# Seeding the last output group in PSUM, a shorter chain to the last root, and smaller stores

## The chip, the cores and the metric

The kernel runs on one core of one Trainium2 chip. The metric is the time of one execution on the device in microseconds (us), as the median of several runs. Engines are called PE (TensorE, matrix products), DVE (VectorE), ACT (ScalarE), POOL (GpSimd) and SP (SyncE, which only issues transfers here). SBUF is the on-chip memory, PSUM the accumulators that PE writes into, 8 banks of 512 float32 columns on 128 partitions.

## What is computed

Two layers over x (256 rows of 2048 features, float32): a gated differential attention, then a gated Conformer convolution, each added to x, and one RMSNorm at the end. Only the last lines matter here:

```
# layer 1, the convolution's output projection, with its bias
y = (u * silu(z)) @ w_out + b_out            # [256, 2048] @ [2048, 2048] + [2048]
x = x + y
# the final norm
out = x * rsqrt(mean(x * x, axis=-1) + 1e-6) * final_gain
```

## The kernel before

The program is one block with a hand-written instruction stream for each engine; semaphores tie them together, and nothing is reordered by a scheduler. float32 products are made of three fast ones: each operand is split into a high part (ScalarE copies it to the type float32r) and a low part (the rest), and `project` issues hi x hi, hi x lo and lo x hi for every 128-row slice of the contraction.

Weights come in chunks of 4 slices by 512 columns (1 MB) through a ring of 4 slots. For each chunk SP loads `w_raw`, ACT writes `w_hi` (L422) once PE has freed the slot (`w_free`), and the low part `w_lo` is made by DVE in the first part of the program and by POOL from chunk `POOL_FROM` on (L413), so in the whole output projection of the convolution. Four chunks make one group of 512 output columns (`GW`); `PAIRS` is 4, so w_out has the groups n = 0 to 3. `acc` has 4 banks: group n uses the banks 2*(n%2) and 2*(n%2)+1, one for each row tile st (rows 0 to 127, and 128 to 255). A group is 96 products: 4 chunks, 4 slices, 2 row tiles, 3 products.

The end of the program, around which the change lies, runs so on each engine:

- DVE, loop over n = 0 to 3: add the output bias to the residual in `xs` (L982, both row tiles: two operands in SBUF, result in SBUF). Then for n < 3: wait until PE has finished group n, add `acc` to `xs` (L990), wait for ACT's sum of squares, and multiply by the final gain (L995, again two operands in SBUF). For n = 3, once for each row tile: add `acc` (L1004), multiply by the gain into `gained_rows` (L1006), add up the four sums of squares (L1009), scale and add epsilon (L1010), wait for ACT's root, take the reciprocal (L1013), scale the column groups 0 and 1 (L1017).
- ACT: high parts of the chunks (L422), the squares of each finished group with a sum (L685, `squares_of_y`), and at the end for each row tile the root (L697) and the scaling of the groups 2 and 3 (L701).
- PE: the groups 0 to 2 with both row tiles in each chunk, where group n >= 2 waits for `y_ready` (the banks emptied by DVE). Group 3 is written out apart: first all four chunks for row tile 0, then all four for row tile 1, so that the end of row tile 0 runs beside the products of row tile 1. The first product of a bank has `start=True`, which overwrites; the others add to what the bank holds.
- SP: the stores of the output, two for each row tile, 1024 columns (512 KB) each (L387).

The waits of group 3 on PE before:

```
pe.wait_ge(y_ready, 2 * (PAIRS - 2))
for st in range(ST):
    for i in range(NCH):
        if st == 0:
            low_part_ready(pe, CHUNKS - NCH + i)
```

Of the kernel before, what the change touches and what calls it, by code (L numbers as in the profile page):

```python
# [21 lines left out]
F32 = mybir.dt.float32  # L22
# [4 lines left out]
P = 128  # L27
# [48 lines left out]
def build(nc, x, x_turned, vectors, taps, final_gain, rel_bias, attn_w_in, attn_w_out, conv_w_in,  # L76
          conv_w_out, conv_b_out, onehot, out):
    with ExitStack() as ctx:  # L78
# [74 lines left out]
        with ExitStack() as one:  # L153
            b_out_bc = sb("b_out_bc", [P, D], F32, one)
            gain_bc = sb("gain_bc", [P, D], F32, one)
            gained_rows = sb("gained_rows", [P, ST, GW], F32, one)
            junk = sb("junk", [P, ST, GW], F32, one)
# [159 lines left out]
        def _(sp):  # L317
# [66 lines left out]
            for st in range(ST):  # L384
                for ready, cols in ((out_ready, slice(0, D // 2)), (out_ready_act, slice(D // 2, D))):
                    sp.wait_ge(ready, 2 * (st + 1))
                    sp.dma_start(out_rows[:, st, cols], xs[:, st, cols]).then_inc(out_stored, 16)  # L387
            sp.wait_ge(out_stored, 16 * PAIRS)
# [29 lines left out]
        def _(act):  # L418
# [269 lines left out]
            for i in range(NCH * PAIRS):  # L688
                if i:
                    hi_of(CHUNKS_CONV + i + RING)  # L690
                if i % NCH == NCH - 1 and i < NCH * (PAIRS - 1):
                    for st in range(ST):
                        squares_of_y(i // NCH, st)
            for st in range(ST):
                squares_of_y(PAIRS - 1, st)
                act.wait_ge(ms_ready, 3 + st)
                act.activation(sd[:, st:st + 1], ms[:, st:st + 1], ACT.Sqrt).then_inc(sd_ready, 1)  # L697
                act.wait_ge(rstd_ready, 4 + st)
                for n in (2, 3):
                    src = xs[:, st, n * GW:(n + 1) * GW] if n < PAIRS - 1 else gained_rows[:, st]  # L700
                    act.activation(xs[:, st, n * GW:(n + 1) * GW], src, ACT.Copy, scale=rstd[:, st:st + 1]  # L701
                                   ).then_inc(out_ready_act, 1)


        @block.vector
        def _(dve):
# [270 lines left out]

            dve.wait_ge(final_landed, 32)
            for n in range(PAIRS):
                for st in range(ST):  # L980
                    cols = xs[:, st, n * GW:(n + 1) * GW]
                    dve.tensor_tensor(cols, cols, b_out_bc[:, n * GW:(n + 1) * GW], ALU.add  # L982
                                      ).then_inc(y_ready_pre, 1)
                if n == PAIRS - 1:
                    break
# [12 lines left out]

            n = PAIRS - 1
            dve.wait_ge(y_ready_pre, 2 * PAIRS)  # L1000
            for st in range(ST):
                cols = xs[:, st, n * GW:(n + 1) * GW]
                dve.wait_ge(rows_done, st + 1)
                dve.tensor_tensor(cols, acc[:, 2 * (n % 2) + st], cols, ALU.add).then_inc(y_ready, 1)  # L1004
                dve.wait_ge(y_ready, 2 * n + st + 1)
# [255 lines left out]
```

## Time and profile before

| | |
|---|---|
| Time, 3 runs | 893.44, 894.64, 894.86 us; median 894.64 |
| Span of the profiled execution | 890.2 us (its own time is not listed apart; the median of the runs is 4.4 us above the span) |
| PE busy | 871.8 us, 98% |
| DVE, ACT, POOL busy | 65%, 51%, 30% of the span |
| Mean granted clock of PE | 0.995 of full speed |

The profile is of one execution. Times are counted from the first instruction; busy time leaves out waits on semaphores, but a DVE instruction that is under way and held up counts as busy for as long as it is held. The granted clock is the share of full speed that PE was given in a stretch: 1.00 is 2.4 GHz and 0.50 is 1.2 GHz. A wait is put down to the engine whose signal came last.

### The profile page before, as it was taken

The page shows a single profiled execution, that of the slowest core. Times are in us where ns is not written, and L with a number is a line of the kernel's source. Part 1 is how long each engine was busy: PE and PEld are TensorE (multiplying, and loading weights), DVE is VectorE, ACT ScalarE, POOL GpSimd, SP SyncE. Part 2 cuts the span into 40 slices and gives each one's busy share as a digit, 9 for nine tenths or more (in the row PEclk, how much of TensorE's full clock was granted, in tenths as well). Part 3 has the DMA queues.
Part 4 walks back from the last instruction along what each step waited for, and adds up shares of the span by engine and source line. Part 5 has one row for each costly group of instructions (what it writes and reads, how often), then busy time and mean ns, then how long its engine had stood idle before and what let it go on. Part 6 is the DMA issues. An engine that isn't in the chain of part 4 may idle for free.

```text
span 890.2 us, 10496 instructions
## 1 busy us (share of the span) xinstructions
PE 871.8 (98%) x3968; PEld 708.1 (80%) x3968; DVE 577.1 (65%) x888; ACT 452.1 (51%) x583; POOL 262.7 (30%) x70
## 2 busy tenths in 40 slices
PE   8999999999999999999999999999999999988996
PEld 7788888888888888888888888888888888866875
DVE  6457544574448544576445536989988899495693
ACT  7746543546445633556444544544454455665532
POOL 0000000000000000000000017777777777647890
PEclk9999999999999999999999999999999999999998
DMA  9976566565664566544555455555555555436522
GB/s 325 395 257 216 160 208 179 181 172 177 188 185 136 159 198 189 181 150 142 190 188 185 146 189 187 173 167 183 189 172 163 185 189 186 146 103 237 191 83 95
DMA packets 97267, 163.54 MB, mean 184 GB/s; under 512 B 3232, under 2 KB 38304, under 8 KB 96712
## 3 DMA queue, kind: packets, MB, share of 16 engines
q1 hardware_dynamic: 96032, 161.29, 55.6%
q10 hardware_dynamic: 1192, 1.67, 0.5%
q8 instruction: 28, 0.46, 0.2%
q14 instruction: 15, 0.12, 0.0%
HBM read 160.83 MB, written 3.69 MB: 185 GB/s over the span
## 4 chain that ended last, share of the span: by engine, by line
issue 76%; POOL 20%; PE 2%; POOLq 1%; ACT 0%; DVE 0%; ACTq 0%
POOL sb_w_lo L413 20%; POOLq L78 1%; PE ps_acc L1060 1%; PE ps_acc L1062 1%; PE ps_acc L1061 1%; POOLq L412 0%; POOLq L410 0%; ACT sb_junk L685 0%; ACT sb_xs L701 0%; DVE sb_xs L1004 0%; ACTq L78 0%; POOLq L413 0%; POOL sb_ident L402 0%; POOL sb_uT L408 0%; ACT sb_small L697 0%
## 5 line engine op out<-in xcount | busy, mean ns | idle before, releaser
L422 ACT ACTIVATE sb_w_hi<-sb_w_raw 128x2048 fp32r<-128x2048 f32 x141 | 269.5, 1914 | 254.1 <-PE ps_acc L1062 244.8
L717 DVE TENSOR_TENSOR sb_w_lo<-sb_w_raw,sb_w_hi 128x2048 fp32r<-128x2048 f32 x85 | 194.7, 2291 | 155.6 <-ACT sb_w_hi L422 155.4
L413 POOL TENSOR_TENSOR sb_w_lo<-sb_w_raw,sb_w_hi 128x2048 fp32r<-128x2048 f32 x56 | 261.2, 4671 | 107.7 <-ACT sb_w_hi L422 107.7
L1060 PE MATMUL ps_acc<-sb_w_hi,sb_act_hi 128*128 128x512 f32 x640 | 254.4, 397 | 2.1 <-DVE sb_w_lo L753 2.1
L1062 PE MATMUL ps_acc<-sb_w_hi,sb_act_lo 128*128 128x512 f32 x640 | 252.6, 395 | 0.0
L1061 PE MATMUL ps_acc<-sb_w_lo,sb_act_hi 128*128 128x512 f32 x640 | 252.6, 395 | 0.0
L1060 PE MATMUL ps_acc<-sb_w_hi,sb_conv_hi 128*128 128x512 f32 x512 | 206.0, 402 | 6.9 <-DVE sb_conv_lo L960 5.8
L1062 PE MATMUL ps_acc<-sb_w_hi,sb_conv_lo 128*128 128x512 f32 x512 | 203.1, 397 | 0.0
L1061 PE MATMUL ps_acc<-sb_w_lo,sb_conv_hi 128*128 128x512 f32 x512 | 203.1, 397 | 0.0
L897 DVE SCALAR_TENSOR_TENSOR ps_d<-sb_uT,sb_dwT,ps_d 128x256 f32<-128x256 f32 x480 | 190.0, 485 | 0.0
L407 POOL MEMSET sb_uT<- 128x240 f32 x1 | 0.3, 307 | 497.1 <-PE ps_acc L1062 497.1
L1060 PEld LDWEIGHTS ps_acc<-sb_w_hi,sb_act_hi 128*128 128x128 f32 x640 | 120.0, 188 | 31.3 <-DVE sb_w_lo L753 2.4
L1062 PEld LDWEIGHTS ps_acc<-sb_w_hi,sb_act_lo 128*128 128x128 f32 x640 | 119.9, 187 | 29.4
L1061 PEld LDWEIGHTS ps_acc<-sb_w_lo,sb_act_hi 128*128 128x128 f32 x640 | 120.1, 188 | 27.9
L1060 PEld LDWEIGHTS ps_acc<-sb_w_hi,sb_conv_hi 128*128 128x128 f32 x512 | 96.7, 189 | 30.2 <-DVE sb_conv_lo L960 6.6
L1062 PEld LDWEIGHTS ps_acc<-sb_w_hi,sb_conv_lo 128*128 128x128 f32 x512 | 96.7, 189 | 23.3
L1061 PEld LDWEIGHTS ps_acc<-sb_w_lo,sb_conv_hi 128*128 128x128 f32 x512 | 96.7, 189 | 21.7
L911 DVE SCALAR_TENSOR_TENSOR sb_uT<-ps_a,sb_vec_all,sb_uT 128x256 f32<-128x256 f32 x16 | 7.8, 485 | 30.3 <-ACT sb_uT L286 30.1
L982 DVE TENSOR_TENSOR sb_xs<-sb_xs,sb_b_out_bc 128x512 f32<-128x512 f32 x8 | 18.9, 2402 | 8.4 <-DMA sb_gain_bc<-in_final_gain 8.4
L490 ACT ACTIVATE sb_qk_rows<-ps_acc,sb_small 128x512 f32<-128x512 f32 x16 | 10.1, 683 | 25.8 <-PE ps_acc L1062 25.4
L484 ACT ACTIVATE sb_q_hi<-ps_a 128x512 fp32r<-128x512 f32 x16 | 8.7, 595 | 28.1 <-PE ps_a L1023 28.1
L995 DVE TENSOR_TENSOR sb_xs<-sb_xs,sb_gain_bc 128x512 f32<-128x512 f32 x6 | 18.4, 3098 | 2.9 <-ACT sb_junk L685 2.9
(142 smaller groups left out, 531.5 us busy)
## 6 DMA issues: line engine op xcount, KB each, us to landing
sb_w_raw<-in_attn_w_in SPq DMA_DIRECT2D x61, 1024.0 KB, 5.4
sb_w_raw<-in_conv_w_in SPq DMA_DIRECT2D x64, 512.0 KB, 4.5
sb_w_raw<-in_attn_w_out SPq DMA_DIRECT2D x16, 1024.0 KB, 5.0
sb_w_raw<-in_conv_w_in SPq DMA_DIRECT2D x16, 1024.0 KB, 5.2
sb_w_raw<-in_conv_w_out SPq DMA_DIRECT2D x16, 1024.0 KB, 5.2
sb_w_raw<-in_attn_w_in SPq DMA_DIRECT2D x6, 512.0 KB, 8.7
sb_xT<-in_x_turned SPq DMA_DIRECT2D x4, 512.0 KB, 8.7
sb_xs<-in_x SPq DMA_DIRECT2D x2, 1024.0 KB, 15.8
```

The costliest lines, as they stand in the source:

```text
L78: with ExitStack() as ctx:
L413: pool.tensor_tensor(w_lo[slot][:], w_raw[slot][:], w_hi[slot][:].bitcast(F32), ALU.subtract).then_inc(lo_ready_pool, 1)
L422: act.activation(w_hi[slot][:], w_raw[slot][:], ACT.Copy).then_inc(hi_ready, 1)
L484: act.activation(dst, bank_a[par][:], ACT.Copy).then_inc(part_hi, 1)
L490: act.activation(dst[:, st], acc[:, 2 * par + st], func, scale=scale[:, st:st + 1]).then_inc(acc_free, 1)
L717: dve.tensor_tensor(w_lo[slot][:], w_raw[slot][:], w_hi[slot][:].bitcast(F32), ALU.subtract).then_inc(lo_ready, 1)
L897: dve.scalar_tensor_tensor(out_, src, dwT[:, k, tap:tap + 1], out_, ALU.mult, ALU.add).then_inc(tap_done, 1)
L982: dve.tensor_tensor(cols, cols, b_out_bc[:, n * GW:(n + 1) * GW], ALU.add).then_inc(y_ready_pre, 1)
L995: dve.tensor_tensor(cols, cols, gain_bc[:, n * GW:(n + 1) * GW], ALU.mult).then_inc(gained, 1)
L1060: pe.matmul(into, left_hi, w_hi[i][:, k], start=(kt == 0), stop=False)
L1061: pe.matmul(into, left_hi, w_lo[i][:, k], start=False, stop=False)
L1062: ins = pe.matmul(into, left_lo, w_hi[i][:, k], start=False, stop=(kt == KT - 1))
```

## The change

1. Group 3 is seeded. DVE no longer adds the bias to `xs` for n = 3 behind group 2; it writes residual plus bias straight into the two PSUM banks of group 3 (helper `with_bias`, new L988), right behind the same operation for n = 2 and after group 1 was taken out of these banks. PE's products of group 3 then all add (`filled=True`: no `start`), and PE waits for all eight `with_bias` operations before the first of them. What PE leaves in the banks is the finished x of these columns.
2. The last root follows its square on ACT. The mean of the groups 0 to 2 with epsilon is made ahead of time (L1013, L1014). For n = 3 ACT takes the square straight from PSUM (L699), and the root takes that sum with a scale and the other groups' mean as its bias (L702). DVE takes the reciprocal (L1018) and then does `acc` x root x gain for group 3 in one instruction (L1020), and scales group 0 (L1023); ACT scales the groups 1 and 2 (L708). `gained_rows`, L1004, L1006 and the reduction behind the last square are gone.
3. Stores have 512 columns (256 KB): four for each row tile, three of them issued by SP in the order 3, 1, 0 and that of group 2 by ACT.

```diff
--- before.py
+++ after.py
@@ -153,7 +153,6 @@
         with ExitStack() as one:
             b_out_bc = sb("b_out_bc", [P, D], F32, one)
             gain_bc = sb("gain_bc", [P, D], F32, one)
-            gained_rows = sb("gained_rows", [P, ST, GW], F32, one)
             junk = sb("junk", [P, ST, GW], F32, one)
 
 
@@ -382,10 +381,12 @@
                     sp.dma_start(gain_bc[:], bass.AP(final_gain.tensor, final_gain.offset, [[0, P], [1, D]])
                                  ).then_inc(final_landed, 16)
             for st in range(ST):
-                for ready, cols in ((out_ready, slice(0, D // 2)), (out_ready_act, slice(D // 2, D))):
-                    sp.wait_ge(ready, 2 * (st + 1))
+                for n, ready, count in ((3, out_ready, 2 * st + 1), (1, out_ready_act, 2 * st + 1),
+                                        (0, out_ready, 2 * st + 2)):
+                    cols = slice(n * GW, (n + 1) * GW)
+                    sp.wait_ge(ready, count)
                     sp.dma_start(out_rows[:, st, cols], xs[:, st, cols]).then_inc(out_stored, 16)
-            sp.wait_ge(out_stored, 16 * PAIRS)
+            sp.wait_ge(out_stored, 16 * ST * PAIRS)
 
 
         @block.gpsimd
@@ -691,15 +692,23 @@
                 if i % NCH == NCH - 1 and i < NCH * (PAIRS - 1):
                     for st in range(ST):
                         squares_of_y(i // NCH, st)
+            last = PAIRS - 1
+            act.wait_ge(ms_ready, 2 + ST)
             for st in range(ST):
-                squares_of_y(PAIRS - 1, st)
-                act.wait_ge(ms_ready, 3 + st)
-                act.activation(sd[:, st:st + 1], ms[:, st:st + 1], ACT.Sqrt).then_inc(sd_ready, 1)
+                act.wait_ge(rows_done, st + 1)
+                act.activation(junk[:, st], acc[:, 2 * (last % 2) + st], ACT.Square,
+                               accum_out=ss[:, 4 * st + last:4 * st + last + 1]).then_inc(ss_ready, 1)
+                act.wait_ge(ss_ready, ST + 2 * PAIRS + 2 * last + st + 1)
+                act.activation(sd[:, st:st + 1], ss[:, 4 * st + last:4 * st + last + 1], ACT.Sqrt, scale=1.0 / D,
+                               bias=ms[:, st:st + 1]).then_inc(sd_ready, 1)
                 act.wait_ge(rstd_ready, 4 + st)
-                for n in (2, 3):
-                    src = xs[:, st, n * GW:(n + 1) * GW] if n < PAIRS - 1 else gained_rows[:, st]
-                    act.activation(xs[:, st, n * GW:(n + 1) * GW], src, ACT.Copy, scale=rstd[:, st:st + 1]
+                for n in (1, 2):
+                    cols = slice(n * GW, (n + 1) * GW)
+                    act.wait_ge(gained, 2 * n + st + 1)
+                    act.activation(xs[:, st, cols], xs[:, st, cols], ACT.Copy, scale=rstd[:, st:st + 1]
                                    ).then_inc(out_ready_act, 1)
+                act.wait_ge(out_ready_act, 2 * st + 2)
+                act.dma_start(out_rows[:, st, cols], xs[:, st, cols]).then_inc(out_stored, 16)
 
 
         @block.vector
@@ -975,14 +984,19 @@
                     gate_block(b + 1)
 
 
+            def with_bias(n, st, dst):
+                dve.tensor_tensor(dst, xs[:, st, n * GW:(n + 1) * GW], b_out_bc[:, n * GW:(n + 1) * GW], ALU.add
+                                  ).then_inc(y_ready_pre, 1)
+
+            last = PAIRS - 1
             dve.wait_ge(final_landed, 32)
-            for n in range(PAIRS):
+            for n in range(last):
                 for st in range(ST):
-                    cols = xs[:, st, n * GW:(n + 1) * GW]
-                    dve.tensor_tensor(cols, cols, b_out_bc[:, n * GW:(n + 1) * GW], ALU.add
-                                      ).then_inc(y_ready_pre, 1)
-                if n == PAIRS - 1:
-                    break
+                    with_bias(n, st, xs[:, st, n * GW:(n + 1) * GW])
+                if n == last - 1:
+                    for st in range(ST):
+                        dve.wait_ge(y_ready, 2 * (n - 1) + st + 1)
+                        with_bias(last, st, acc[:, 2 * (last % 2) + st])
                 dve.wait_ge(w_free, RING + CHUNKS_CONV + NCH * (n + 1))
                 for st in range(ST):
                     cols = xs[:, st, n * GW:(n + 1) * GW]
@@ -995,26 +1009,19 @@
                     dve.tensor_tensor(cols, cols, gain_bc[:, n * GW:(n + 1) * GW], ALU.mult
                                       ).then_inc(gained, 1)
 
-
-            n = PAIRS - 1
-            dve.wait_ge(y_ready_pre, 2 * PAIRS)
             for st in range(ST):
-                cols = xs[:, st, n * GW:(n + 1) * GW]
-                dve.wait_ge(rows_done, st + 1)
-                dve.tensor_tensor(cols, acc[:, 2 * (n % 2) + st], cols, ALU.add).then_inc(y_ready, 1)
-                dve.wait_ge(y_ready, 2 * n + st + 1)
-                dve.tensor_tensor(gained_rows[:, st], cols, gain_bc[:, n * GW:(n + 1) * GW], ALU.mult
-                                  ).then_inc(gained, 1)
-                dve.wait_ge(ss_ready, ST + 2 * PAIRS + 2 * n + st + 1)
-                link(dve.tensor_reduce(ms[:, st:st + 1], ss[:, 4 * st:4 * st + 4], AX.X, ALU.add))
+                link(dve.tensor_reduce(ms[:, st:st + 1], ss[:, 4 * st:4 * st + last], AX.X, ALU.add))
                 dve.tensor_scalar(ms[:, st:st + 1], ms[:, st:st + 1], 1.0 / D, EPS, ALU.mult, ALU.add
                                   ).then_inc(ms_ready, 1)
+            for st in range(ST):
                 dve.wait_ge(sd_ready, 3 + st)
                 dve.reciprocal(rstd[:, st:st + 1], sd[:, st:st + 1]).then_inc(rstd_ready, 1)
                 dve.wait_ge(rstd_ready, 4 + st)
-                for m in range(PAIRS // 2):
-                    out_cols = xs[:, st, m * GW:(m + 1) * GW]
-                    dve.tensor_scalar(out_cols, out_cols, rstd[:, st:st + 1], None, ALU.mult).then_inc(out_ready, 1)
+                dve.scalar_tensor_tensor(xs[:, st, last * GW:], acc[:, 2 * (last % 2) + st], rstd[:, st:st + 1],
+                                         gain_bc[:, last * GW:], ALU.mult, ALU.mult).then_inc(out_ready, 1)
+                dve.wait_ge(gained, st + 1)
+                dve.tensor_scalar(xs[:, st, 0:GW], xs[:, st, 0:GW], rstd[:, st:st + 1], None, ALU.mult
+                                  ).then_inc(out_ready, 1)
 
 
         @block.tensor
@@ -1048,7 +1055,7 @@
                                    rows[:, st, kt * P:(kt + 1) * P])
                 ins.then_inc(d_full, 1)
 
-            def project(i, par, hi, lo, halfway=None, tiles=range(ST), done=w_free):
+            def project(i, par, hi, lo, halfway=None, tiles=range(ST), done=w_free, filled=False):
 
                 for k in range(CK):
                     if k == CK // 2 and halfway:
@@ -1057,9 +1064,11 @@
                     for st in tiles:
                         into = acc[:, 2 * par + st]
                         left_hi, left_lo = hi[:, kt, st * P:(st + 1) * P], lo[:, kt, st * P:(st + 1) * P]
-                        pe.matmul(into, left_hi, w_hi[i][:, k], start=(kt == 0), stop=False)
-                        pe.matmul(into, left_hi, w_lo[i][:, k], start=False, stop=False)
-                        ins = pe.matmul(into, left_lo, w_hi[i][:, k], start=False, stop=(kt == KT - 1))
+                        pe.matmul(into, left_hi, w_hi[i][:, k], start=(kt == 0 and not filled), stop=False,
+                                  skip_group_check=filled)
+                        pe.matmul(into, left_hi, w_lo[i][:, k], start=False, stop=False, skip_group_check=filled)
+                        ins = pe.matmul(into, left_lo, w_hi[i][:, k], start=False, stop=(kt == KT - 1),
+                                        skip_group_check=filled)
                 if done:
                     ins.then_inc(done, 1)
 
@@ -1221,13 +1230,13 @@
                     conv_fill(pe, turn, kind, m, f)
 
 
-            pe.wait_ge(y_ready, 2 * (PAIRS - 2))
+            pe.wait_ge(y_ready_pre, 2 * PAIRS)
             for st in range(ST):
                 for i in range(NCH):
                     if st == 0:
                         low_part_ready(pe, CHUNKS - NCH + i)
                     project(i, (PAIRS - 1) % 2, conv_hi, conv_lo, tiles=(st,),
-                            done=rows_done if i == NCH - 1 else None)
+                            done=rows_done if i == NCH - 1 else None, filled=True)
 
 
 def kernel(**inputs):
```

**DVE, from the gain of group 1 (L995 before, L1009 now) to the gain of group 2**, before (`ps_acc` are the banks, L982 the bias, L990 the addition of the group that PE finished):

```order
L995 TENSOR_TENSOR sb_xs<-sb_xs,sb_gain_bc 128x512 [waits ss_ready] x2
L982 TENSOR_TENSOR sb_xs<-sb_xs,sb_b_out_bc 128x512 x2
L990 TENSOR_TENSOR sb_xs<-ps_acc,sb_xs 128x512 [waits y_ready_pre,w_free]
L990 TENSOR_TENSOR sb_xs<-ps_acc,sb_xs 128x512 [waits y_ready_pre]
L995 TENSOR_TENSOR sb_xs<-sb_xs,sb_gain_bc 128x512 [waits ss_ready] x2
L982 TENSOR_TENSOR sb_xs<-sb_xs,sb_b_out_bc 128x512 x2
```

and now:

```order
L1009 TENSOR_TENSOR sb_xs<-sb_xs,sb_gain_bc 128x512 [waits ss_ready] x2
L988 TENSOR_TENSOR sb_xs<-sb_xs,sb_b_out_bc 128x512 x2
L988 TENSOR_TENSOR ps_acc<-sb_xs,sb_b_out_bc 128x512 [waits y_ready] x2
L1004 TENSOR_TENSOR sb_xs<-ps_acc,sb_xs 128x512 [waits y_ready_pre,w_free]
L1004 TENSOR_TENSOR sb_xs<-ps_acc,sb_xs 128x512 [waits y_ready_pre]
L1009 TENSOR_TENSOR sb_xs<-sb_xs,sb_gain_bc 128x512 [waits ss_ready] x2
```

The pair for group 3 has moved from the end of this stretch to a place ahead of the addition of group 2, and its output is PSUM.

**ACT, from the last squares of group 2 to the end of row tile 0**, before (the third of the squares in the first row is group 3's):

```order
L685 ACTIVATE sb_junk,sb_small<-sb_xs 128x512 [waits ss_ready,y_ready] x3
L697 ACTIVATE sb_small<-sb_small 128x1 [waits ms_ready]
L701 ACTIVATE sb_xs<-sb_xs,sb_small 128x512 [waits rstd_ready]
L701 ACTIVATE sb_xs<-sb_gained_rows,sb_small 128x512
```

and now:

```order
L686 ACTIVATE sb_junk,sb_small<-sb_xs 128x512 [waits ss_ready,y_ready] x2
L699 ACTIVATE sb_junk,sb_small<-ps_acc 128x512 [waits rows_done,ms_ready]
L702 ACTIVATE sb_small<-sb_small 128x1 [waits ss_ready]
L708 ACTIVATE sb_xs<-sb_xs,sb_small 128x512 [waits gained,rstd_ready]
L708 ACTIVATE sb_xs<-sb_xs,sb_small 128x512 [waits gained]
L711 DMA out_x<-sb_xs 128x512 [waits out_ready_act]
```

The square waits for PE itself (`rows_done`), the root for the square, and a store stands behind the two copies.

## Rows read from the trace of the kernel before

**Rows 1.** The page: busy time of each engine, share of the span, instructions.

```profile
PE 871.8 (98%) x3968; PEld 708.1 (80%) x3968; DVE 577.1 (65%) x888; ACT 452.1 (51%) x583; POOL 262.7 (30%) x70
```

**Rows 2.** The chain that ended last, from 882 us: start, length, what.

```profile
882.43 0.25 PE ps_acc L1062
...
882.70 0.70 DVE sb_xs L1004
...
883.42 0.73 ACT sb_junk L685 x2
...
884.18 0.17 DVE sb_small L1009
...
884.37 0.17 DVE sb_small L1010
...
884.56 0.21 ACT sb_small L697
...
884.99 0.72 ACT sb_xs L701
```

**Rows 3.** Timeline of PE, group 3: start, length, line, products, [idle before <- who].

```profile
858.71 0.39 PE L1060 MATMUL ps_acc<-sb_w_hi,sb_conv_hi 128*128 128x512 f32 x1
...
866.87 0.40 PE L1062 MATMUL ps_acc<-sb_w_hi,sb_conv_lo 128*128 128x512 f32 x1
868.40 0.50 PE L1060 MATMUL ps_acc<-sb_w_hi,sb_conv_hi 128*128 128x512 f32 x1 [1.13 <-POOL sb_w_lo L413]
...
882.26 0.40 PE L1062 MATMUL ps_acc<-sb_w_hi,sb_conv_lo 128*128 128x512 f32 x1
```

**Rows 4.** Timelines of POOL from 825 us and of its last operation, same columns.

```profile
829.42 38.93 POOL L413 TENSOR_TENSOR sb_w_lo<-sb_w_raw,sb_w_hi 128x2048 fp32r<-128x2048 f32 x8 [4.41 <-ACT sb_w_hi L422]
...
863.33 5.02 POOL L413 TENSOR_TENSOR sb_w_lo<-sb_w_raw,sb_w_hi 128x2048 fp32r<-128x2048 f32 x1
```

**Rows 5.** Timeline of DVE, 839 to 870 us, same columns.

```profile
839.12 9.68 DVE L995 TENSOR_TENSOR sb_xs<-sb_xs,sb_gain_bc 128x512 f32<-128x512 f32 x2 [1.33 <-ACT sb_junk L685]
848.73 10.13 DVE L982 TENSOR_TENSOR sb_xs<-sb_xs,sb_b_out_bc 128x512 f32<-128x512 f32 x2
858.90 1.29 DVE L990 TENSOR_TENSOR sb_xs<-ps_acc,sb_xs 128x512 f32<-128x512 f32 x2
861.53 7.37 DVE L995 TENSOR_TENSOR sb_xs<-sb_xs,sb_gain_bc 128x512 f32<-128x512 f32 x2 [1.33 <-ACT sb_junk L685]
868.82 1.28 DVE L982 TENSOR_TENSOR sb_xs<-sb_xs,sb_b_out_bc 128x512 f32<-128x512 f32 x2
```

**Rows 6.** Timeline of DVE, 864 to 868 us: the second of the two L995.

```profile
863.83 5.06 DVE L995 TENSOR_TENSOR sb_xs<-sb_xs,sb_gain_bc 128x512 f32<-128x512 f32 x1
```

**Rows 7.** Timeline of PE around an earlier idle stretch, 788 to 794 us.

```profile
788.47 0.51 PE L1060 MATMUL ps_acc<-sb_w_hi,sb_conv_hi 128*128 128x512 f32 x1 [2.96 <-DVE sb_conv_lo L960]
...
789.51 0.57 PE L1061 MATMUL ps_acc<-sb_w_lo,sb_conv_hi 128*128 128x512 f32 x1
...
793.28 0.48 PE L1060 MATMUL ps_acc<-sb_w_hi,sb_conv_hi 128*128 128x512 f32 x1
```

**Rows 8.** PE by windows: us, PE busy (count), granted clock, DMA share, GB/s.

```profile
790.00:792.00 2.00, 2.00 (x6) 0.50 1.05 408
```

**Rows 9.** All engines by windows: PE, PEld, DVE, ACT, POOL busy, clock, DMA, GB/s.

```profile
885.00:886.00 1.00, 0.00 (x0) 0.00 (x0) 0.88 (x2) 1.00 (x2) 0.00 (x0) 0.57 0.00 0
...
887.00:888.00 1.00, 0.00 (x0) 0.00 (x0) 0.00 (x0) 0.00 (x0) 0.00 (x0) 0.50 1.00 401
```

**Rows 10.** Timeline of the end: DVE's scaling of two groups, SP's two stores.

```profile
884.99 0.88 DVE L1017 TENSOR_SCALAR sb_xs<-sb_xs,sb_small 128x512 f32<-128x512 f32 x2
...
885.90 0.81 SPq L387 DMA_DIRECT2D out_x<-sb_xs  x2
```

**Rows 11.** Transfers, 885 to 890 us: issuer, count, size, us from issue to landing.

```profile
out_x<-sb_xs SPq DMA_DIRECT2D x2, 512.0 KB, 3.1
```

**Rows 12.** Groups by line and form, whole span: busy, mean ns, idle before.

```profile
L801 DVE SCALAR_TENSOR_TENSOR sb_v_lo<-ps_acc,sb_small,sb_v_hi 128x512 fp32r<-128x512 f32 x8 | 5.6, 745 | 0.0
```

## The prediction

> **What bounds the kernel now.** I read the page first: PE is busy for 98% of the span, all others for at most 65% [rows 1]. So a change counts where it moves PE's last product, or what comes behind it. The chain that ended last shows the second part: PE ends at 882.7 us, and then DVE and ACT hand one small result to each other until the first scaled columns exist, 0.70 + 0.73 + 0.17 + 0.17 + 0.21 us and so on up to the copy at 884.99 [rows 2]. From PE's end to the end of the span at 890.2 it is 7.5 us.
>
> PE's timeline gives the first part. Group 3 starts at 858.71, right behind group 2: 36 products (three chunks for row tile 0) at 0.233 us each bring it to 867.1, then PE waits 1.3 us for POOL's last low part and goes on at 868.40, 60 products to 882.66 [rows 3]. Group 3 thus has 22.65 us of work, and its start hangs on nothing that is late.
>
> Then I looked at who works beside it. POOL makes eight low parts back to back from 829.42 to 868.35, about 4.9 us each [rows 4]. In the same stretch DVE's rows read strangely. An addition of 512 columns takes 0.64 us when POOL rests (two in 1.28 at 868.82). While POOL works, the two L995 take 9.68, the two L982 take 10.13, and of the next two L995 the second alone takes 5.06 [rows 5, 6], which is one operation of POOL (5.02, [rows 4]). But the two L990 at 858.90 take 1.29, in the middle of POOL's work [rows 5]. What tells them apart is the inputs: L982 and L995 read two operands from SBUF, L990 one from PSUM and one from SBUF; all write SBUF. So a DVE operation with two SBUF inputs gets through only once per operation of POOL. It costs nothing today: the pair L982 ends at 858.86, just as PE ends group 2.
>
> **The change part by part.**
>
> *Seeding group 3.* The new pair L988 reads `xs` and the bias, both in SBUF, and stands behind the pair for n = 2, so it starts at 858.86. POOL still has the operation under way (to 863.3) and the last one (to 868.35). I take one of the pair per operation of POOL, as for the two L995 that stood in exactly this place and ended at 868.89 [rows 5, 6]. The new wait is PE's: it needs both before its first product of group 3. What is queued behind it is all of group 3, 96 products; what it frees is nothing, since low parts 0 to 2 have long been there. PE starts at 868.89 plus 0.04 for the signal, 868.93, and has its 22.65 us of work ahead: end at 891.58 where it was 882.66. The old wait for POOL (1.3 us) is gone in this sum, since POOL is done by then. **Term: +8.9.** No row shows a DVE operation with two SBUF inputs and an output in PSUM, so bounds: if the output decides, the pair takes 1.3 us and PE starts at 860.2 (term +0.2, a rival below); the upper end is +8.9, since POOL has no work behind 868.35. I take the upper end, as all held rows differ from L990 in an input and in no output.
>
> The Trainium skill, page "SBUF — State Buffer", section "Who interferes with whom", says that a DVE instruction with two SBUF inputs contends with a GpSimd instruction that reads SBUF because its second input comes through the shared read interface, and that whoever has it keeps it for the whole instruction. It speaks of inputs only, so by it the output in PSUM changes nothing, and it speaks against this change: by it the sum is that of this forecast, by a rule on outputs it would be 893.6. The rows on L982, L995 and L990 agree with it.
>
> *PE's clock.* PE now idles from 858.7 to 868.9, 10.2 us. Behind the last product at 882.66 the granted clock reads 0.57 in the window from 885 on and 0.50 later [rows 9]: some 2.8 us without work bring it down to 1.2 GHz. So PE restarts at the low clock. For the way back there is one case: after an idle stretch of about 3 us PE restarts at 788.47, runs slow from 789.51 to 793.28 (3.8 us; 0.50 in the window from 790 [rows 8]), and its products then come 0.43 apart, not 0.233 [rows 7]. 3.8 us at 0.43 hold 8.8 products that need 2.1 us at full speed: a loss of 1.7. Lower end 0 (no fall, or back at once). Upper end: slow from the restart on for the 4.8 us that it took there until 793.28, a loss of 2.2. **Term: +1.7**, the case seen.
>
> *The end.* Before, 0.04 + 0.70 (L1004) + 0.02 + 0.73 (square) + 0.19 + 0.19 (L1009, L1010 with their gaps) + 0.23 (root) + 0.19 (reciprocal) lead to the scaling, 0.88 for both groups on DVE, and the first store is issued at 885.90, 3.24 behind PE's end [rows 2, 10]. Now: square 0.76 from PE's end on, root 0.23, reciprocal 0.19, then L1020, for which I take the 0.75 of the nearest form, PSUM x factor with another SBUF operand [rows 12], and 0.04: first store at 1.97. That is 1.27 less: L1004, L1009 and L1010 leave the path, and the first store waits for one instruction of 0.75 instead of 0.88. The last store is issued at about 2.8 instead of 3.67: ACT's second copy ends near 2.6, SP's third issue follows at some 0.4 each (two in 0.81 [rows 10]). That is 0.87 less. What has to leave stays 1 MB per row tile, at 401 GB/s [rows 9] 2.6 us, and starts 1.27 earlier. **Term: -1.2**; lower end of the gain 0.5 (two more issues in full on the path), upper end 1.9 (1.27 and the last 256 KB less behind the last issue). L1013 and L1014 for the mean of three groups run while PE is in row tile 0, and so do the addition, the squares and the gain of group 2, which move behind the pair to 868.9 and need some 4 us: cover is the 11 us of row tile 0, and nobody waits for these banks. The store of group 2 waits on ACT for ACT's own copies; behind it stands only the square of row tile 1, 11 us later. In row tile 0 the same saving lies beside PE's work and is worth nothing.
>
> For stores only a page has a price by size: the Trainium skill, "DMA: Bandwidth & Descriptors", section "Anatomy of one DMA — SWDGE (gpsimd) path", gives about 2.0 us fixed and the bytes at 436 GB/s. For 512 KB that makes 3.2 and the trace has 3.1 from issue to landing [rows 11]; by it a store of 256 KB lands 0.6 sooner, the gain would be an estimated 1.5 and the total 903.7.
>
> **Sum.** +8.9 + 1.7 - 1.2 = +9.4 on a span of 890.2, so about 899.6; the median of the runs is 4.4 above the span, and I keep that: 894.64 + 9.4 = **904.0 us**, 1.0% slower.
>
> **Rivals.** A measurement of this kernel can tell about 0.2% (1.8 us) from no change.
>
> 1. *The seed is not held (ends on the other side).* If the output decides, or an output in PSUM spares the pair, it takes 1.29 like L990. PE starts at 860.2; after 36 products it is at 868.6, and POOL's last low part at 868.4 is there, so only 0.2 is lost, the clock stays up, and the end gains 1.2: 893.6, with the upper end of the gain 892.9. It decides at one point: whether the new L988 reads 0.65 or 5. For it: no row has this form. Against it: the inputs sort all rows. Chance 0.07, of which 0.02 for more than 0.2% faster.
> 2. *Only one of the pair is held*, because both slip in between two operations of POOL. PE starts at about 863.9: +3.9 + 1.7 - 1.2, 899.0. Against it: the pairs of 9.68 and 10.13 each took two operations of POOL. Chance 0.04.
> 3. *The clock does not fall*, or is back at once: 902.3. Chance 0.06.
> 4. *The clock stays low for all of group 3*: 96 products by 0.19, +19 instead of +1.7: 921. The one case in the trace was over in 4.8 us. Chance 0.03.
>
> **The numbers.** The forecast has 0.80. The range is 900.5 to 907.0: the lower ends of clock and store gain (8.9 - 1.9 = +7.0, and 1.1 for the spread of the runs of before), the upper ends (8.9 + 2.2 - 0.5 = +10.6) and 1.8 for a slow stretch longer than the one seen. It takes in rival 3. Slower 0.93 (forecast, rivals 2 to 4), same 0.05, faster 0.02.
>
> **What would show it.** Right: the new L988 with `ps_acc` as output as two rows of about 5 us, the last ending near 868.9; the first product of group 3 directly behind it, with an idle time of some 10 us put down to DVE; a granted clock of 0.50 in the windows from 869 to 872; PE's end near 893; the first store some 2 us behind it. Wrong: an L988 pair of 1.3 us, or group 3 starting near 860. If PE's end is right and the total is not, the end was mis-sized.

## The result and the profile after

| | before | changed |
|---|---|---|
| Time, median (lowest to highest) | 894.06 us (893.44 to 894.86, 4 runs) | 904.80 us (904.48 to 904.98, 4 runs) |
| Ratio | | 1.0122, 95% interval 1.011 to 1.0135 |
| Span of the profiled execution | 890.2 us | 903.2 us |
| Last product of PE to the end of the span | 7.5 us | 7.2 us |

The change makes the kernel 10.7 us slower. The forecast was 904.0 us, with a range of 900.5 to 907.0.

The seed is where the time went. DVE's timeline of the changed kernel around group 3 (start, length, line, out<-in, count; the second fence is a window that begins inside the pair, so the second one stands alone, beside POOL's last low part):

```profile
851.34 10.15 DVE L988 TENSOR_TENSOR sb_xs<-sb_xs,sb_b_out_bc 128x512 f32<-128x512 f32 x2
861.41 9.95 DVE L988 TENSOR_TENSOR ps_acc<-sb_xs,sb_b_out_bc 128x512 f32<-128x512 f32 x2
871.27 1.27 DVE L1004 TENSOR_TENSOR sb_xs<-ps_acc,sb_xs 128x512 f32<-128x512 f32 x2
872.74 1.31 DVE L1009 TENSOR_TENSOR sb_xs<-sb_xs,sb_gain_bc 128x512 f32<-128x512 f32 x2 [0.19 <-ACT sb_junk L686]
```

```profile
865.86 4.95 POOL L414 TENSOR_TENSOR sb_w_lo<-sb_w_raw,sb_w_hi 128x2048 fp32r<-128x2048 f32 x1
866.38 4.98 DVE L988 TENSOR_TENSOR ps_acc<-sb_xs,sb_b_out_bc 128x512 f32<-128x512 f32 x1
```

These answer to [rows 4 to 6]: the pair that writes PSUM is held as long as the pair that writes SBUF, one of them per operation of POOL, and the last ends 0.55 us behind POOL's last. PE's timeline shows who waits for it:

```profile
862.69 0.39 PE L1070 MATMUL ps_acc<-sb_w_hi,sb_conv_lo 128*128 128x512 f32 x1
871.41 0.79 PE L1067 MATMUL ps_acc<-sb_w_hi,sb_conv_hi 128*128 128x512 f32 x1 [8.33 <-DVE ps_acc L988]
872.00 0.63 PE L1069 MATMUL ps_acc<-sb_w_lo,sb_conv_hi 128*128 128x512 f32 x1
...
875.42 0.49 PE L1067 MATMUL ps_acc<-sb_w_hi,sb_conv_hi 128*128 128x512 f32 x1
875.75 0.39 PE L1069 MATMUL ps_acc<-sb_w_lo,sb_conv_hi 128*128 128x512 f32 x1
...
895.57 0.39 PE L1070 MATMUL ps_acc<-sb_w_hi,sb_conv_lo 128*128 128x512 f32 x1
```

The first products come 0.43 apart, from 875.4 on 0.233. The windows by one microsecond (PE, weight loads, DVE, ACT and POOL busy, granted clock, DMA share, GB/s) have the clock beside it:

```profile
870.00:871.00 1.00, 0.00 (x0) 0.00 (x0) 1.00 (x1) 0.00 (x0) 0.80 (x1) 0.50 0.00 0
872.00:873.00 1.00, 1.00 (x4) 0.80 (x3) 0.81 (x2) 1.00 (x3) 0.00 (x0) 0.50 0.00 0
875.00:876.00 1.00, 1.00 (x5) 0.82 (x4) 0.00 (x0) 0.00 (x0) 0.00 (x0) 0.69 0.00 0
876.00:877.00 1.00, 1.00 (x6) 0.82 (x5) 0.00 (x0) 0.00 (x0) 0.00 (x0) 1.00 0.00 0
```

Group 3 takes 24.56 us from its first product (871.41) to its end (895.97), where 96 products at full speed are 22.65: the low clock costs 1.9.

The spans are 13.0 apart and the times only 10.7. In every execution that is listed with both, the time is some 1.8 us above the span, so the profile of before (890.2) shows an execution of about 892.0 us (an estimate), 2.1 below the median. The 4.4 us between span and median in front of the prediction are these 1.8 and the distance of that one execution from the median. The rows show where it was faster: POOL's last low part ends at 870.81 here and at 868.35 before, 2.5 later, through something that the change doesn't touch. Near the program's start PE ran partly at the low clock in this profile and not in the other. Windows of PE (busy, count, granted clock, DMA share, GB/s), of the kernel before:

```profile
10.00:20.00 10.00, 10.00 (x45) 1.00 1.05 396
```

and of the changed kernel:

```profile
10.00:20.00 10.00, 10.00 (x34) 0.73 1.05 391
```

Counted from the end of POOL's last low part, PE ends 14.31 us later before (882.66) and 25.16 later now (895.97): 10.85 is what the seed cost.

The end became only a little shorter. Chain of the changed kernel behind PE's last product (start, length, what):

```profile
896.00 0.70 ACT sb_junk L699 x2
...
896.72 0.30 ACT sb_small L702
...
897.05 0.17 DVE sb_small L1018
```

Timelines of DVE, SP and ACT behind that:

```profile
897.25 0.75 DVE L1020 SCALAR_TENSOR_TENSOR sb_xs<-ps_acc,sb_small,sb_gain_bc 128x512 f32<-128x512 f32 x1
...
898.03 1.30 SPq L388 DMA_DIRECT2D out_x<-sb_xs  x3
```

```profile
898.61 0.34 ACTq L711 DMA_DIRECT2D out_x<-sb_xs  x1
```

The first store leaves 2.06 behind PE's end, where it was 3.24 [rows 10]. But the stores then move slower. Windows of the last transfers, and the landing times of all eight stores:

```profile
899.00:900.00 1.00, 0.00 (x0) 0.00 (x0) 0.00 (x0) 0.00 (x0) 0.00 (x0) 0.76 1.07 375
900.00:901.00 1.00, 0.00 (x0) 0.00 (x0) 0.00 (x0) 0.00 (x0) 0.00 (x0) 0.50 1.05 318
901.00:902.00 1.00, 0.00 (x0) 0.00 (x0) 0.00 (x0) 0.00 (x0) 0.00 (x0) 0.50 0.87 297
```

```profile
DMA to landing us min/median/max: 2.5/3.3/4.0
```

With the transfer engines fully busy (shares of 1.07 and 1.05) these stores moved 375 and then 318 GB/s, where stores of 1024 columns had 401 [rows 9].

### The profile page after: what moved, and what is told of

It is laid out like the page before. It is cut to its first block, busy times and chain, and to the rows that moved or that the text cites. A ratio compares the mean times of both kernels' runs of the same rounds, so it can differ in the third digit from the quotient of the medians.

```text
span 903.2 us, 10496 instructions
## 1 busy us (share of the span) xinstructions
PE 878.0 (97%) x3968; PEld 711.7 (79%) x3968; DVE 575.5 (64%) x884; ACT 452.6 (50%) x583; POOL 262.5 (29%) x70
## 4 chain that ended last, share of the span: by engine, by line
PE 91%; DVE 4%; issue 2%; ACT 2%; DMA 1%; ACTq 0%
PE ps_acc L1067 28%; PE ps_acc L1070 28%; PE ps_acc L1069 28%; PE ps_a L1030 3%; DVE ps_acc L988 1%; DVE sb_xs L1009 1%; PE ps_d L1030 1%; DVE sb_conv_lo L969 1%; DVE sb_xs L988 1%; DVE sb_uT L965 1%; DMA sb_vec_all<-in_vectors 1%; ACT sb_uT L613 0%; PE ps_a L1136 0%; PE ps_d L1113 0%; PE ps_a L1135 0%
## 5 line engine op out<-in xcount | busy, mean ns | idle before, releaser
L988 DVE TENSOR_TENSOR sb_xs<-sb_xs,sb_b_out_bc 128x512 f32<-128x512 f32 x6 | 17.5, 2964 | 8.5 <-DMA sb_gain_bc<-in_final_gain 8.5
L800 DVE TENSOR_TENSOR sb_probs<-ps_d,sb_bias_w 128x512 f32<-128x512 f32 x16 | 11.0, 688 | 12.9 <-PE ps_d L1113 12.9
```

Of the source, the lines that this page charges most:

```text
L800: dve.tensor_tensor(probs[:, hq], bank_d[hq % 2][:].rearrange("p (c s) -> p c s", c=2), window, ALU.add).then_inc(d_free, 1)
L988: dve.tensor_tensor(dst, xs[:, st, n * GW:(n + 1) * GW], b_out_bc[:, n * GW:(n + 1) * GW], ALU.add).then_inc(y_ready_pre, 1)
```

## The experiments

Each is timed beside the kernel before, on one chip per group of four, and compared with it. Beside the first four (no seed to PE kept busy) the kernel before had a median of 893.59 us (19 runs), beside the other four 893.67 (35 runs); the 894.06 in the table are from the four runs beside the changed kernel. The ratio is an estimate over all runs of both kernels, not the quotient of two medians. "End" is the time from PE's last product to the end of the span in the profile.

| run | median, us | ratio to before, 95% | PE's wait ahead of group 3 or for POOL | end, us |
|---|---|---|---|---|
| before | 894.06 | 1 | 1.1 (POOL) | 7.5 |
| changed | 904.80 | 1.0122 (1.011 to 1.0135) | 8.3 (seed) | 7.2 |
| no seed | 893.17 | 0.9993 (0.9983 to 1.0002) | none | 8.0 |
| one seed operation | 899.49 | 1.0067 (1.005 to 1.0083) | 3.8 (seed) | 7.2 |
| seed moved up | 893.74 | 1.0008 (0.9998 to 1.0017) | 1.6 (POOL) | 7.3 |
| PE kept busy | 902.64 | 1.0107 (1.009 to 1.0124) | 1.7 (seed) | 7.2 |
| moved up, wide stores | 893.04 | 0.9992 (0.9983 to 1.0001) | 1.5 (POOL) | 6.8 |
| before, narrow stores | 894.04 | 1.0000 (0.999 to 1.0009) | none | 8.1 |
| seed with one SBUF input | 894.21 | 1.0001 (0.9992 to 1.0011) | 1.9 (POOL) | 7.3 |
| all together | 893.58 | 0.9992 (0.9983 to 1.0001) | none | 6.4 |

**No seed.** The changed kernel with the bias of group 3 added into `xs` as before; DVE adds `acc` to it behind PE's last product, and the rest of the new end stays, except that ACT's square reads `xs` instead of PSUM. PE's first product of each bank overwrites it again.

```diff
-                if n == last - 1:
-                    for st in range(ST):
-                        dve.wait_ge(y_ready, 2 * (n - 1) + st + 1)
-                        with_bias(last, st, acc[:, 2 * (last % 2) + st])
...
+            for st in range(ST):
+                with_bias(last, st, xs[:, st, last * GW:])
...
+                dve.wait_ge(rows_done, st + 1)
+                dve.tensor_tensor(cols, acc[:, 2 * (last % 2) + st], cols, ALU.add).then_inc(y_ready, 1)
```

> Parts 2 and 3 of the change without the seed: the bias of group 3 is added into xs behind group 2, as before, and DVE takes acc into xs before ACT's square. Theory (the seed pair is held by POOL and PE waits for it): group 3 starts right behind group 2, PE waits for POOL's last low part as before, and the total is 893.5 to 894.6. Rival (the time was lost in the new end or in the stores): about 904.

Measured 893.17, a little below the range that was expected. Without the seed the whole loss is gone. The end takes 8.0 us here, 0.8 more than with the seed, since DVE's addition (0.69) is back on the path.

**One seed operation.** The seed of both row tiles in one DVE operation of 1024 columns.

```diff
-                    for st in range(ST):
-                        dve.wait_ge(y_ready, 2 * (n - 1) + st + 1)
-                        with_bias(last, st, acc[:, 2 * (last % 2) + st])
+                    dve.wait_ge(y_ready, 2 * n)
+                    dve.tensor_tensor(acc[:, 2:4], xs[:, :, last * GW:],
+                                      b_out_bc[:, last * GW:].unsqueeze(1).to_broadcast([P, ST, GW]), ALU.add
+                                      ).then_inc(y_ready_pre, 2)
```

> The seed of both row tiles in one DVE operation of 1024 columns instead of two of 512, in the same place. Theory (a DVE operation with two SBUF inputs gets through once per POOL operation, whatever its size): it ends one POOL operation earlier, PE starts some 4.4 us earlier than in the changed kernel, total about 900.3. Rival (DVE and POOL share the bandwidth, so the cost goes by columns): it takes the same 10 us and the total stays at 904.8.

Measured 899.49. Its DVE timeline:

```profile
861.15 5.57 DVE L998 TENSOR_TENSOR ps_acc<-sb_xs,sb_b_out_bc 128x1024 f32<-128x1024 f32 x1
```

The same 1024 columns take 5.57 us in one operation and 9.95 in two. So the hold goes by operations and not by data: each waits for the POOL operation under way and then runs at its own speed (5.57 is 0.6 more than 4.98, for the second 512 columns). This speaks against a bandwidth that the two engines share. POOL's next operation is held in turn:

```profile
865.59 5.55 POOL L414 TENSOR_TENSOR sb_w_lo<-sb_w_raw,sb_w_hi 128x2048 fp32r<-128x2048 f32 x1
```

It takes 5.55, where POOL's operations in this profile took 4.99 to 5.08 behind one of 512 columns and 4.60 to 4.61 behind none. In this profile the low clock cost more than in that of the changed kernel: group 3 takes 24.98 us (866.78 to 891.76), 2.3 more than at full speed.

**Seed moved up.** The seed pair directly behind the addition of group 1, ahead of group 1's gain and group 2's bias (the counts of `y_ready_pre` that others wait for are moved with it).

```diff
+                if n == last - 2:
+                    for st in range(ST):
+                        dve.wait_ge(y_ready, 2 * n + st + 1)
+                        with_bias(last, st, acc[:, 2 * (last % 2) + st])
...
-            pe.wait_ge(y_ready_pre, 2 * PAIRS)
+            pe.wait_ge(y_ready_pre, 2 * PAIRS - 2)
```

> The changed kernel with the seed pair moved up on DVE: directly behind the addition of group 1, ahead of group 1's gain and group 2's bias. Theory (only the place of the pair in DVE's queue is at fault): the pair is still held, about 5 us each, but ends some 10 us before PE needs it; group 2's additions come late instead and nobody waits; total 893.4 to 894.3. Rival (the seed itself, or products that add to a seeded bank, cost time): above 895.

Measured 893.74. The seeds, and then group 2's additions and gains, in its DVE timeline:

```profile
839.36 6.53 DVE L988 TENSOR_TENSOR ps_acc<-sb_xs,sb_b_out_bc 128x512 f32<-128x512 f32 x2
845.80 10.12 DVE L1009 TENSOR_TENSOR sb_xs<-sb_xs,sb_gain_bc 128x512 f32<-128x512 f32 x2
855.85 10.12 DVE L988 TENSOR_TENSOR sb_xs<-sb_xs,sb_b_out_bc 128x512 f32<-128x512 f32 x2
865.89 1.27 DVE L1000 TENSOR_TENSOR sb_xs<-ps_acc,sb_xs 128x512 f32<-128x512 f32 x2
```

Seven operations with two SBUF inputs are now stretched by POOL, the first of them only to 1.5 us, where six were before the change. But the seeds are in place at 845.9, some 15 us ahead of group 3, and the late ones are those that nobody waits for. The seed itself and products that add to a seeded bank cost nothing that these times can show (the interval reaches from -0.02% to 0.17%).

**PE kept busy.** The changed kernel with products ahead of PE's wait whose result nobody reads.

```diff
+            for _ in range(70):
+                pe.matmul(bank_d[1][:, 0:SEQ], conv_hi[:, 0, 0:P], conv_hi[:, 0], start=True, stop=True)
             pe.wait_ge(y_ready_pre, 2 * PAIRS)
```

> The changed kernel with 70 products of 256 columns, whose result nobody reads, ahead of PE's wait for the seed, so that PE works through most of it. Theory (1.9 us of the loss are group 3's slow start at the low clock): granted clock 1.00 in the first 4 us of group 3, total about 902.9. Rival (the low clock costs nothing that counts): 904.8.

Measured 902.64, 2.2 less than the changed kernel. PE's timeline:

```profile
860.12 8.55 PE L1234 MATMUL ps_d<-sb_conv_hi 128*128 128x256 f32 x70
870.37 0.50 PE L1067 MATMUL ps_acc<-sb_w_hi,sb_conv_hi 128*128 128x512 f32 x1 [1.70 <-DVE ps_acc L988]
870.70 0.40 PE L1069 MATMUL ps_acc<-sb_w_lo,sb_conv_hi 128*128 128x512 f32 x1
...
892.63 0.40 PE L1070 MATMUL ps_acc<-sb_w_hi,sb_conv_lo 128*128 128x512 f32 x1
```

Group 3 now takes 22.66 us, with a granted clock of 1.00 throughout: the 1.9 of the low clock are gone, but group 3 still starts 0.6 behind POOL's last low part.

**Seed with one SBUF input.** The bias of group 3 goes into `xs` early, behind the bias of group 1; the seed in the changed kernel's place is then `xs` times 1.0.

```diff
+                if n == 1:
+                    for st in range(ST):
+                        link(dve.tensor_tensor(xs[:, st, last * GW:], xs[:, st, last * GW:],
+                                               b_out_bc[:, last * GW:], ALU.add))
...
-                        with_bias(last, st, acc[:, 2 * (last % 2) + st])
+                        dve.tensor_scalar(acc[:, 2 * (last % 2) + st], xs[:, st, last * GW:], 1.0, None, ALU.mult
+                                          ).then_inc(y_ready_pre, 1)
```

> The changed kernel with the bias of group 3 added into xs while POOL rests (behind the bias of group 1), so that the seed in the changed kernel's place is an operation with one SBUF input: xs times 1.0 into PSUM. Theory (the second SBUF input is what POOL holds up, not the output in PSUM): the two seeds take under 0.8 us each in the middle of POOL's work, PE starts within 2 us of group 2's end, total 893.4 to 894.6. Rival (an output in PSUM, or any access from SBUF, is held): 5 us each and 904.8.

Measured 894.21. In its DVE timeline the bias of group 2 is held and the seeds behind it are not, in the middle of POOL's eight operations (830.73 to 870.59):

```profile
846.41 10.13 DVE L988 TENSOR_TENSOR sb_xs<-sb_xs,sb_b_out_bc 128x512 f32<-128x512 f32 x2
856.47 1.27 DVE L1003 TENSOR_SCALAR ps_acc<-sb_xs 128x512 f32<-128x512 f32 x2
```

The place and the output are the same and there is one SBUF input less: 0.6 each instead of 5. The operation is also another one (TENSOR_SCALAR for TENSOR_TENSOR), but a TENSOR_TENSOR with one input from PSUM and one from SBUF passes in the same way, 1.29 for two [rows 5]. The bias of group 3 did not quite find POOL at rest, as had been expected: the second of its two operations took 5.01 us, from 831.40 on, beside POOL's first. Nobody waited for it.

**Stores.** Three runs on the end. First the kernel with the seed moved up and stores of 1024 columns:

```diff
-                for n, ready, count in ((3, out_ready, 2 * st + 1), (1, out_ready_act, 2 * st + 1),
-                                        (0, out_ready, 2 * st + 2)):
-                    cols = slice(n * GW, (n + 1) * GW)
-                    sp.wait_ge(ready, count)
+                for half, act_count, dve_count in ((0, 1, 2), (1, 2, 2)):
+                    cols = slice(half * D // 2, (half + 1) * D // 2)
+                    sp.wait_ge(out_ready_act, 2 * st + act_count)
+                    sp.wait_ge(out_ready, 2 * st + dve_count)
...
```

Both stores come from SP; ACT's is gone.

> The kernel with the seed pair moved up, but with two stores of 1024 columns per row tile, both from SP, instead of four of 512. The end from PE's last product to the end of the span took 7.24 us with four stores of 512 columns in every profile with the new end, and 7.5 before. Theory (stores of 512 columns give back most of what the shorter chain to the root gained): 6.8 us or less, total 893.2. Rival (what gave it back is on the engines, as ACT's and DVE's copies): 7.2 or more.

Measured 893.04 (0.9992, interval 0.9983 to 1.0001), and an end of 6.8 us (last product's end at 883.00, span 889.8). Its first store leaves 0.4 later behind PE's end than the changed kernel's, at 2.49, and it still ends 0.4 sooner.

The kernel before with four stores of 512 columns per row tile:

```diff
-                for ready, cols in ((out_ready, slice(0, D // 2)), (out_ready_act, slice(D // 2, D))):
-                    sp.wait_ge(ready, 2 * (st + 1))
+                for n, ready, count in ((0, out_ready, 2 * st + 1), (2, out_ready_act, 2 * st + 1),
+                                        (1, out_ready, 2 * st + 2), (3, out_ready_act, 2 * st + 2)):
+                    cols = slice(n * GW, (n + 1) * GW)
+                    sp.wait_ge(ready, count)
...
```

> The kernel before with its four outputs per row tile stored as four pieces of 512 columns by SP, nothing else changed. Theory (rows of 2 KB move slower and the last pieces land later): from PE's last product to the end of the span 7.8 to 8.3 us instead of 7.5, the transfer itself 3.2 instead of 2.7, total within 0.1% of before. Rival (smaller stores start earlier and win): 7.2 or less.

Measured 894.04, no difference in time that can be told; the end is 8.1 us instead of 7.5. The windows of its last transfers:

```profile
889.00:890.00 1.00, 0.00 (x0) 0.00 (x0) 0.00 (x0) 0.26 (x1) 0.00 (x0) 0.62 0.74 277
890.00:891.00 1.00, 0.00 (x0) 0.00 (x0) 0.00 (x0) 0.00 (x0) 0.00 (x0) 0.50 1.10 336
891.00:892.00 1.00, 0.00 (x0) 0.00 (x0) 0.00 (x0) 0.00 (x0) 0.00 (x0) 0.50 1.06 322
892.00:893.00 1.00, 0.00 (x0) 0.00 (x0) 0.00 (x0) 0.00 (x0) 0.00 (x0) 0.50 0.32 115
```

So smaller stores alone are a small loss at the end, about 0.6 us, in the kernel before too: the shares of these windows add up to 3.2 us for 1 MB, where they are 2.6 in the profile of before. The times don't show the 0.6. All eight stores come from SP here, so the second issuer is not the cause; whether it is the shorter rows or the larger number of stores, no run separates.

Last, the seed moved up and stores of 1024 columns together with two more edits that no run had tried alone: group 0 scaled ahead of group 3, and the gains of the groups 1 and 2 behind POOL's last low part.

```diff
...
+                if n == 1:
+                    continue
+                if n == last - 1:
+                    dve.wait_ge(lo_ready_pool, CHUNKS - POOL_FROM)
+                for m in ((0,) if n == 0 else (1, 2)):
                     for st in range(ST):
...
```

> Seed pair moved up, stores of 1024 columns, DVE scales group 0 ahead of group 3 so that the first store can leave earlier, and the gains of the groups 1 and 2 wait until POOL's last low part is done, so that only four DVE operations instead of eight compete with POOL's last eight. Theory: POOL's eight low parts take some 38 us instead of 39.3, PE's wait for the last one shrinks from 1.6 to below 1, and the end takes some 6.4 us: total about 892, 0.2% under the kernel before. Rival (the end is bound by the transfer of 1 MB and its landing whatever the stores): 893.2.

Measured 893.58, with an end of 6.4 us as expected, but no clear gain in time (0.9992, interval 0.9983 to 1.0001): the 892 that were expected were missed. POOL's eight operations took 38.5 instead of 39.3, with four operations of DVE held beside them instead of seven. In this profile that bought nothing, since PE was late by itself and did not wait for POOL at all. The reason stands in the windows from 814 us on, behind PE's wait for the convolution's last low parts (`sb_conv_lo`), which the change leaves alone. Of this kernel:

```profile
814.00:816.00 2.00, 2.00 (x6) 1.58 (x5) 0.00 (x0) 0.00 (x0) 2.00 (x1) 0.50 0.72 193
816.00:818.00 2.00, 2.00 (x7) 1.57 (x6) 0.00 (x0) 0.00 (x0) 2.00 (x2) 0.65 1.06 422
```

and of the kernel with the seed moved up, where the clock stays up behind the same wait:

```profile
814.00:816.00 2.00, 2.00 (x10) 1.61 (x9) 0.00 (x0) 0.19 (x1) 2.00 (x1) 1.00 0.94 373
```

Of the ten profiles, five have the low clock in this place, and in these five PE does not wait for POOL later. In four of the other five it waits for POOL, 1.1 to 1.9 us. In the changed kernel the low clock makes group 2 end 1.7 later, counted from PE's restart behind that wait (49.4 instead of 47.7 before). But from the restart to PE's last product it is 71.8 us in the three profiles with the low clock and no seed to wait for, and 71.7 to 72.6 in the four with the full clock. So either the low clock or the wait for POOL is paid, and 0.8 taken from POOL can show only where the clock stays up.

## Why the prediction was right, point by point

**The held seed (+8.9): right in mechanism and size.** PE started 0.60 us behind the end of POOL's last low part; the forecast had 868.93 against 868.35, 0.58. Removing the seed (893.17), moving it (893.74) and taking one SBUF input from it (894.21) each bring the time back to before, and halving the number of operations gives back half. One reading was off without touching the term: the forecast gave PE 10.2 us of idle time, and it had 8.3, mostly because group 2 ended 1.7 later behind the low clock at 814; the start of group 3 hangs on POOL and DVE alone. By the Trainium skill, "SBUF — State Buffer", section "Who interferes with whom", a DVE instruction with two SBUF inputs contends with GpSimd's reads and the shared ports are an exclusive lock. That the holder keeps them for the whole instruction, as the prediction has it, the Trainium skill writes there of DVE's 2-port modes. The rows here agree for two inputs too: one input passes (1.27 us for two operations), 1024 columns wait and then run (5.57), and POOL's operation behind them is held in turn (5.55).

**The low clock (+1.7): right, measured 1.9** in the profile and 2.2 in the times with PE kept busy. With one seed operation it was 2.3, a little above the 2.2 that the forecast had as its upper end: one earlier case did not give the spread of this term. The forecast also read the fall of the clock at PE's end as 2.8 us behind the last product; 0.57 in the window from 885 on puts it at 885.1, 2.5 behind. No term uses it.

**The end (-1.2): the step that was mis-sized.** It measured -0.3 (7.5 to 7.2), outside the bounds that I gave it (0.5 to 1.9). The chain to the first store came out as worked out, 1.18 shorter where I had 1.27; the root with its bias from a column took 0.30 instead of 0.21. What failed is the sentence that what has to leave "stays 1 MB per row tile, at 401 GB/s": that rate belongs to stores of 1024 columns, and with 512 it was 375 and 318 in the two full windows, some 0.5 us more for the 1 MB (the shares add up to 3.15 us instead of 2.63); a piece took up to 4.0 us to land instead of 3.5. The narrow stores in the kernel before show the same loss (0.6) without the rest of the change. The price by size from the Trainium skill, "DMA: Bandwidth & Descriptors", section "Anatomy of one DMA — SWDGE (gpsimd) path", erred further in the same direction: its fixed time and rate gave an estimated gain of 1.5, and the Trainium skill fits them to transfers that GpSimd issues, while these come from SP and ACT.

**The sum.** 8.9 + 1.9 - 0.3 = 10.5 against 10.7 measured; the forecast of 9.4 was low by the 0.9 of the end and the 0.2 of the clock. That the forecast time lay only 0.8 below the measured one is partly luck: it was counted from 894.64, and the kernel before came out at 894.06.

**The rivals.** That the output in PSUM spares the seed fell: the row reads 9.95 for the pair. That both slip in between two operations of POOL fell too; one operation per POOL operation holds in every DVE timeline shown here. The clock did fall (rival 3) and was back 4.0 us after the restart (rival 4).

**What the change could have brought.** With the seed in a harmless place and wide stores the end falls from 7.5 to 6.8, and to 6.4 with the first store released sooner. In the times it is 0.08%, with an interval that takes in no change. No version was shown to beat the kernel before; the effect of the shorter chain alone, with the stores of before and without a seed, was not timed.

## What to carry to other kernels

An operation moved off the last chain has a price in its new place, and its length there is read from the rows of that stretch, not from the rows of the quiet end: 0.64 us there were 5 here. Before a queue's operation becomes something that PE waits for, sort the slow and fast rows of its neighbours by operands; a second SBUF input beside a busy POOL was the whole difference. Another order or one input less takes the cost away; one long operation in place of two halves it. And give a store's rate only for the row length that it was read at.

## What the runs showed of the hardware that was not expected

- PE's wait that ends between 811 and 814 us was followed by the low clock in five of ten profiles and not in the other five, with no change to the code there. The length of the wait does not sort them: the clock stayed up behind 2.8 us in five profiles and fell behind 2.8 us in two and behind 1.9 in three. The five are the ones whose granted clock was 0.73 to 0.75 in the window from 10 to 20 (0.86 to 1.00 in the others); what ties the two together is not shown.
- That low clock near the start moves everything behind it: PE restarts from this wait at 813.5 to 813.8 in these five, at 811.0 in the two profiles with 1.00 there, and at 812.3 to 812.7 in the three between. The later one is hidden by the wait for POOL, as shown above. Two spans should not be subtracted without looking at the start.
- The changed kernel's four times lie within 0.5 us of each other, those of before and of the variants within 1.2 to 3.4. Most of those are from more runs, and two variants that also wait for the seed have 1.5 and 1.8 with four, so four runs may simply have fallen close together.
- Stores of rows of 2 KB moved at 307 to 375 GB/s in windows with the transfer engines fully busy, those of rows of 4 KB at 401. Loads of weights in packets of 2 KB (398 packets, 0.82 MB) moved at 408 in the window from 790 to 792 of the kernel before [rows 8], so packets of this size are not slow as such.
